# First mixer of a two-block transformer kernel: eight modulation chunks multiplied and summed on VectorE, with TensorE summing over partitions only

## What is computed

```python
mod = (silu(c) @ w_mod + b_mod).reshape(bsz, 6, 1024)      # for x
mc = (silu(c_ctx) @ w_mod + b_mod).reshape(6, 1024)        # for ctx, only mc[0] and mc[1] are used
hc = modulate(rmsnorm(ctx, g_mix), mc[0], mc[1])           # -> forget gates, values -> two start states
h = modulate(rmsnorm(x, g_mix), mod[:, 0], mod[:, 1])
mix_x = token_mixers(h @ w_in, ..., start states)          # gated linear attention + spatial gating
x = x + mod[:, 2] * mix_x
h2 = modulate(rmsnorm(x, g_ffn), mod[:, 3], mod[:, 4])
x = x + mod[:, 5] * swiglu(h2, w_up, w_down)
```

## Time and profile before

| | |
|---|---|
| runs shown, us | 1447.14, 1448.66, 1449.80 |
| median, us | 1448.66 |
| span of the profiled execution, us | 1447.1 |
| busy share of the span: TensorE, VectorE, ScalarE | 98%, 59%, 53% |
| granted TensorE clock, mean | 0.996 |
| bytes moved by DMA, mean rate | 268.39 MB, 185 GB/s |

### The profile page before, as it was taken

One profiled execution on the slowest core, in us unless ns is written; L12 is line 12 of the kernel. 1 busy time (PEld: TensorE's weight loads), 2 busy tenths in 40 slices (PEclk: granted clock), 3 DMA queues, 4 the chain that ended last, 5 costly groups with the idle time before them and its releaser, 6 DMA issues.

```text
span 1447.1 us, 19624 instructions
## 1 busy us (share of the span) xinstructions
PE 1420.6 (98%) x8042; PEld 1195.6 (83%) x8042; DVE 860.0 (59%) x1205; ACT 766.7 (53%) x1126; POOL 37.1 (3%) x72
## 2 busy tenths in 40 slices
PE   6999999999999999999999999999999999999998
PEld 5898889978888788888997888888888889888886
DVE  3628766875554755556576655557555475765553
ACT  4535355464453654446685655546545376754542
POOL 0000000000000000000241000000000000000000
PEclk9999999999999999999999999999999999999999
DMA  9537666555555556555534555565655551365552
GB/s 386 206 133 277 224 235 211 178 185 182 184 188 189 198 183 186 189 189 192 172 118 146 180 187 189 185 201 182 188 185 182 188 181 60 128 185 184 186 189 88
DMA packets 70074, 268.39 MB, mean 185 GB/s; under 512 B 7776, under 2 KB 8032, under 8 KB 66400
## 3 DMA queue, kind: packets, MB, share of 16 engines
q1 hardware_dynamic: 67968, 261.23, 53.5%
q10 hardware_dynamic: 2016, 5.90, 1.5%
HBM read 266.05 MB, written 1.05 MB: 185 GB/s over the span
## 4 chain that ended last, share of the span: by engine, by line
PE 92%; DVE 3%; ACT 2%; DMA 1%; issue 1%; SPq 0%; POOL 0%; ACTq 0%
PE PS L726 25%; PE PS L742 14%; PE PS L744 14%; PE PS L743 14%; PE PS L379 5%; PE PS L380 4%; PE PS L381 4%; PE PS L710 2%; PE PS L481 1%; PE PS L413 1%; DMA MC<-in_mod 1%; PE PS L414 1%; PE PS L415 1%; DVE WL L1701 1%; PE PS L1001 1%
## 5 line engine op out<-in xcount | busy, mean ns | idle before, releaser
L1701 DVE TENSOR_TENSOR WL<-RAW,WH 128x1024 fp32r<-128x1024 f32 (+1 forms) x440 | 533.8, 1223 | 282.4 <-ACT WH L1101 281.0
L1101 ACT ACTIVATE WH<-RAW 128x1024 fp32r<-128x1024 f32 (+1 forms) x440 | 452.2, 1054 | 263.0 <-DMA RAW<-in_up 134.2
L742 PE MATMUL PS<-WH,XH 128*128 128x512 f32 (+1 forms) x928 | 381.6, 411 | 2.8 <-DVE XL L2150 2.2
L744 PE MATMUL PS<-WH,XL 128*128 128x512 f32 (+1 forms) x928 | 362.8, 391 | 0.0
L743 PE MATMUL PS<-WL,XH 128*128 128x512 f32 (+1 forms) x928 | 362.5, 391 | 0.0
L742 PEld LDWEIGHTS PS<-WH,XH 128*128 128x128 f32 x928 | 174.7, 188 | 52.4 <-DVE XL L2150 5.9
L744 PEld LDWEIGHTS PS<-WH,XL 128*128 128x128 f32 x928 | 174.5, 188 | 37.2
L743 PEld LDWEIGHTS PS<-WL,XH 128*128 128x128 f32 x928 | 175.5, 189 | 27.7
L726 PE MATMUL PS<-WH,GH 128*128 128x512 f32 x440 | 137.8, 394 | 0.0
L726 PE MATMUL PS<-WL,GH 128*128 128x512 f32 x440 | 135.8, 390 | 0.0
L726 PE MATMUL PS<-WH,GL 128*128 128x512 f32 x440 | 135.8, 390 | 0.0
(11 more groups left out here) (351 smaller groups left out, 1832.9 us busy)
## 6 DMA issues: line engine op xcount, KB each, us to landing
RAW<-in_up SPq DMA_DIRECT2D x220, 512.0 KB, 3.6
RAW<-in_down SPq DMA_DIRECT2D x110, 512.0 KB, 3.3
RAW<-in_win SPq DMA_DIRECT2D x36, 512.0 KB, 4.8
RAW<-in_mod SPq DMA_DIRECT2D x16, 1024.0 KB, 6.7
MC<-in_mod SPq DMA_DIRECT2D x8, 1024.0 KB, 11.7
RAW<-in_sbqk SPq DMA_DIRECT2D x16, 512.0 KB, 5.0
GROW<-in_grow ACTq DMA_DIRECT2D x9, 512.0 KB, 4.7
RAW<-in_fg SPq DMA_DIRECT2D x8, 512.0 KB, 8.8
```

The costliest lines, as they stand in the source:

```text
L742: e.matmul(o_[:, 0:n], l, w[:, s], start=(k == 0), stop=False, skip_group_check=True)
L744: m = e.matmul(o_[:, 0:n], ll, w[:, s], start=False, stop=(k == KD - 1), skip_group_check=True)
L1101: e.activation(WH[s][:, 0:c], RAW[s][:, 0:c], ACT.Copy).then_inc(*sig("hi", j))
L1701: e.tensor_tensor(WL[s][:, 0:c], RAW[s][:, 0:c], WH[s][:, 0:c].bitcast(F32), ALU.subtract).then_inc(*sig("lo", j))
```

## The change

Chunks 8 to 15 of the modulation leave the weight plan and the slots. They are loaded in four pairs (8 and 9, 10 and 11, 12 and 13, 14 and 15; `EARLY`) into one buffer ME of 16 KB for each partition. VectorE multiplies the eight row blocks of a pair by the condition, one scalar for each partition, and adds them up in a tile MA of 512 columns (`early_sums`). TensorE sums over the partitions (`early_rows`): one matmul with a matrix of ones for the pairs 8 and 10, four matmuls with slices of MA as the stationary operand for the pairs 12 and 14. VectorE adds the bias (`early_added`). SP loads pair 0 after the gate's chunks and the others after the chunks 14, 17 and 19, each after the sums of the pair before it. ScalarE waits for the last sums before it loads ROW and WST, which lie where ME is. The places of the remaining chunks 16 to 23 among the projections change with it.

```diff
-    nxt = 8
+    late = {11: (16, 17), 13: (18, 19), 15: (20,), 17: (21,), 19: (22,), 20: (23,)}
     for i in range(10, 22):
-        n = 2 if i < 14 else 1
-        plan += [("mod", nxt + z, 2048) for z in range(n)]
-        nxt += n
+        plan += [("mod", n, 2048) for n in late.get(i, ())]
         plan += [("win", 2 * i + z, 1024) for z in range(2)]
...
+        ME = ph("ME", 64, [P, 2, 2048])
+        MA = Ring([ph(f"MA{i}", 60 + 2 * i, [P, 2, T]) for i in range(2)])
+        EARLY = (8, 10, 12, 14)
...
+            def early_rows(i):
+
+                b, empty = bank(("modt", i), ("mod", i))
+                ma = MA.of(("ma", i))
+                pe.wait_ge(*at("ma", i))
+                pe.wait_ge(*empty)
+                if i // 4 == 2:
+                    m = e.matmul(b[:, :], ONE, ma[:, :, :], start=True, stop=True)
+                else:
+                    for t in range(4):
+                        m = e.matmul(b[:, 2 * t:2 * t + 2], ma[:, t // 2, t % 2 * P:t % 2 * P + P], ONE[:, 0:2],
+                                     start=True, stop=True)
+                m.then_inc(*sig("modt", i))
...
-            for c in range(2):
-                token_chunk("win", 4 + c, ("vt", 0, c), ("vc", 0, c), HH, HL, at("hl", 7))
-                token_chunk("win", 4 + c, ("vt", 1, c), ("vc", 1, c), HCH, HCL, at("hcl", 7))
-            for c in range(2):
-                pair("win", 6 + c, ("pl", "Q", c), ("plc", "Q", c), HH, HL, at("hl", 7))
+            token_chunk("win", 4, ("vt", 0, 0), ("vc", 0, 0), HH, HL, at("hl", 7))
+            early_rows(8)
+            token_chunk("win", 4, ("vt", 1, 0), ("vc", 1, 0), HCH, HCL, at("hcl", 7))
+            early_rows(10)
+            token_chunk("win", 5, ("vt", 0, 1), ("vc", 0, 1), HH, HL, at("hl", 7))
+            token_chunk("win", 5, ("vt", 1, 1), ("vc", 1, 1), HCH, HCL, at("hcl", 7))
+            early_rows(12)
+            pair("win", 6, ("pl", "Q", 0), ("plc", "Q", 0), HH, HL, at("hl", 7))
+            pair("win", 7, ("pl", "Q", 1), ("plc", "Q", 1), HH, HL, at("hl", 7))
+            early_rows(14)
...
-            mods(8)
             plain("OG", 0, 10)
-            mods(9)
             gla_scores(0)
-            mods(10)
+            mods(16)
             gla_states(0)
-            mods(11)
+            mods(17)
             plain("OG", 1, 11)
             gla_out(0)
-            mods(12)
             plain("UU", 0, 12)
-            mods(13)
             gla_scores(1)
-            mods(14)
+            mods(18)
             gla_states(1)
-            mods(15)
+            mods(19)
             plain("UU", 1, 13)
...
+            ac.wait_ge(*at("ma", 14))
             for i in range(3):
                 e.dma_start(ROW[:, i, :], a["rows"][i:i + 1, :].to_broadcast([P, 512])).then_inc(s_row, 16)
             e.dma_start(WST[:, :, :], a["wst"]).then_inc(s_row, 16)
...
+            def early_sums(p):
+
+                i = EARLY[p]
+                ma, before = MA.take(("ma", i), ("modt", i))
+                dv.wait_ge(s_early, 32 * (p + 1))
+                dv.wait_ge(*at("act", "silc"))
+                dv.wait_ge(*after(before))
+                for k in range(KD):
+                    w, s = ME[:, :, k * T:(k + 1) * T], SILC[:, k, 0:1]
+                    if k == 0:
+                        e.tensor_scalar(ma[:, :, :], w, s, None, ALU.mult).then_inc(*sig("dve", "ma", i, k))
+                        continue
+                    dv.wait_ge(*at("dve", "ma", i, k - 1))
+                    m = e.scalar_tensor_tensor(ma[:, :, :], w, s, ma[:, :, :], ALU.mult, ALU.add)
+                    m.then_inc(*(sig("dve", "ma", i, k) if k < KD - 1 else sig("ma", i)))
...
             split(9)
+            early_sums(0)
             for src, dst in enumerate((FX, FC)):
...
                 split(14 + src)
-            for c in range(2):
-                split_to("win", 4 + c)
+            early_sums(1)
+            early_added(0)
+            early_sums(2)
+            early_added(1)
+            split_to("win", 4)
+            early_sums(3)
+            split_to("win", 5)
+            early_added(2)
             dv.wait_ge(*at("act", "ln c"))
...
+            def early(p):
+                if p:
+                    sp.wait_ge(*at("ma", EARLY[p - 1]))
+                for z in range(2):
+                    e.dma_start(ME[:, z, :], a["mod"][EARLY[p] + z]).then_inc(s_early, 16)
+
+            early(0)
             for j in range(KD, len(plan)):
                 weights(j)
+                if j in (14, 17, 19):
+                    early({14: 1, 17: 2, 19: 3}[j])
```

More of the change, by code:

```diff
@@ L614, in pe_program @@
                 m.then_inc(*sig("s0", dr))
-            mods(8)
             plain("OG", 0, 10)
-            mods(9)
             gla_scores(0)
-            mods(10)
+            mods(16)
             gla_states(0)
-            mods(11)
+            mods(17)
             plain("OG", 1, 11)
             gla_out(0)
-            mods(12)
             plain("UU", 0, 12)
-            mods(13)
             gla_scores(1)
-            mods(14)
+            mods(18)
             gla_states(1)
-            mods(15)
+            mods(19)
             plain("UU", 1, 13)
-            mods(16)
             gla_out(1)
             plain("GA", 0, 14)
-            mods(17)
+            mods(20)
             plain("GA", 1, 15)
-            mods(18)
             plain("GA", 2, 16)
@@ L648, in pe_program @@
                 m.then_inc(*sig("ob", z))
-            mods(19)
+            mods(21)
             plain("GA", 3, 17)
-            mods(20)
             plain("GB", 0, 18)
@@ L661, in pe_program @@
                 m.then_inc(*sig("sg", g))
-            mods(21)
+            mods(22)
             plain("GB", 1, 19)
-            mods(22)
+            mods(23)
             plain("GB", 2, 20)
-            mods(23)
             plain("GB", 3, 21)
@@ L1746, in mods, with early_added @@
                     split_to("mod", i)
+            def early_sums(p):
[12 more added lines that the diff above has]
+                    m.then_inc(*(sig("dve", "ma", i, k) if k < KD - 1 else sig("ma", i)))
+            def early_added(p):
+                i = EARLY[p]
+                dv.wait_ge(*at("modt", i))
+                b = BANK.of(("modt", i))
+                if i // 4 == 2:
+                    c = slice(i % 4 * T, i % 4 * T + 2 * T)
+                    dv.wait_ge(s_grow[0], 16)
+                    e.tensor_tensor(GROW[0][:, c], b[:, :], GROW[0][:, c], ALU.add).then_inc(*sig("mod", i))
+                else:
+                    e.tensor_tensor(MOD[:, 2 * i:2 * i + 4, :], four(b[:, 0:8]),
+                                    SM[:, S_BMOD + 2 * i:S_BMOD + 2 * i + 4].unsqueeze(2).to_broadcast([P, 4, 2]),
+                                    ALU.add).then_inc(*sig("mod", i))
             def scale_of(name, dst, gcol, mcol, which, n):
@@ L1860, in dve_program @@
             plain(7)
+            early_added(3)
             dv.wait_ge(*at("vt", 1, 1))
```

26 lines of the change are left out of this document (9 added, 17 removed).

## The result

The changed kernel takes 1455.97 us in the median (1455.02 to 1456.45); the kernel before, run beside it on the same chip, 1448.76. The ratio is 1.0049, with a 95% interval of 1.0036 to 1.0061: 7.2 us slower. The profiled execution spans 1453.8 us against 1447.1, 6.7 more.

The account below looks back on a forecast made before the run. TensorE, busy 98% of the span, bounds the kernel; transposes 16.1 us late, less 12.7 of removed matmuls, plus 4.0 of later waits, make +7.4: 1448.66 becomes 1456 us, range 1450 to 1461.

Parts of the forecast that it names:

- TensorE's early rows: Four row sums added on TensorE ahead of the transposes L602: 3.6 us, free if TensorE waits there anyhow.
- VectorE's sums: One multiplication and seven multiply-and-adds on VectorE for each pair of chunks: 6.05 us, 5.4 to 6.6 as bounds.
- Rival C: VectorE's multiply-and-adds take 0.27 us a step, so the loaded pairs finish sooner: -3.3 us, 1445; chance 0.06.
- Chunk 15 behind 2 MB: Chunk 15 queues on SP behind pair 1's load; its low half ends at about 81.9, 82.5 at most.
- The reload: Refilling the single buffer ME after a pair's sums: 8.3 us plus 0.1 for hand-overs, twice on the chain.
- Rival B: Quick refills of ME, 5.3 us each: +1.4 us, 1450, not to be told from no change; chance 0.12.
- ScalarE's queue: ScalarE's loads of ROW and WST wait for the last sums at 116.9, putting the logarithm behind them at 120.1.
- The stop at chunk 17: TensorE idles 8.3 us, from 119.6 to 127.9, in the first value chunk, waiting for chunk 17's low half.
- The clock at the stop: After the idle wait at chunk 17 TensorE runs at half clock for 3.3 us, costing 1.65 us.
- rival A: TensorE's clock stays up through the wait at chunk 17: L602 ends 15.0 late, +6.3 us, 1455; shares chance 0.82.
- The waits after them: After the transposes L602, TensorE waits for KD and KT in both directions: together 4.0 us (2 to 6).
- rival D: Clock falls in short waits too, or a refill of ME takes 9.5 us: +10 to +12, 1460; shares chance 0.82.

## Why the prediction was right, point by point

The forecast, 1456 us and slower, was met with 1455.97. Part of that closeness is luck, since two terms were off in opposite directions.

- **TensorE's loss of work.** By the ledger 12.0 to 12.9 us, 12.3 in the mean; forecast 12.7. Right.
- **TensorE's early rows.** In the two-buffer kernel, where TensorE is hardly waiting ahead of the transposes, and which stands level with the kernel before at 56 us, these start 4.3 us late, of which 0.5 is the wait for the low half. The rest, 3.8, is the early rows with the hand-overs around them; I had 3.6, hidden in the stop. Right.
- **VectorE's sums.** 0.49 and 5.48 us, and 5.9 from a pair's start to the start of what follows it; I had 6.05, and 5.4 to 6.6 as bounds. Rival C, with a step of 0.27 us, is out: seven steps take 5.48, 0.78 each.
- **Chunk 15 behind 2 MB.** Its low half ended at 80.91 + 1.23 = 82.1 in the profiled execution (81.9 forecast). In the other kernels with early pairs it ended between 82.1 and 84.2, in six of ten beyond my bound of 82.5: right here, with too narrow a bound.
- **The reload: mis-sized.** I took 8.3 and 0.1 from a pair of chunks at 125.56. From the first issue to the start of the sums it took 95.26 - 88.08 = 7.2 and 108.65 - 101.28 = 7.4. Two of them make the last sum 2.2 us earlier than said, 114.65 instead of 116.9, and the logarithm with it, 117.80 instead of 120.1; TensorE's wait of 2 us at the last early rows has all but gone. The estimate of 6.8 us from the Trainium skill ("DMA: Bandwidth & Descriptors", Anatomy of one DMA) was nearer than my row: a bound of 7.3 stood in the range, and 8.3 was the wrong end to take it from. Rival B, with 5.3, is out.
- **ScalarE's queue.** From the last sum to the logarithm 117.80 - 114.65 = 3.15 us, forecast 3.2. Right; and the run with the loads behind the logarithm shows that the whole wait on ScalarE is worth 3 to 4 us of the time and not more.
- **The stop at chunk 17.** 8.08 us (forecast 8.3), ended by VectorE's low half. Right.
- **The clock at the stop.** It was at 0.50 from 122 to 128, and had begun to rise between 128 and 130, some 3 us after work resumed. 36 matmuls and their switches took 131.35 - 125.68 = 5.67 us, against 4.54 in the two-buffer kernel (117.67 to 122.21, at a clock of 1.00): 1.1 us, forecast 1.65. Right in kind; rival A is out. Even a clock that stays up wouldn't give all of it back: Pc's second half was ready at 128.93 + 2.37 = 131.30 and no earlier, and with the matmuls in the stop the transposes did wait for it.
- **The transposes.** 13.5 us late and not 16.1: 2.2 from the reloads, the rest from the 36 matmuls (5.67 us, forecast 4.4 + 1.65).
- **The waits after them: mis-sized.** I said 4.0: KD 1.8 and 1.0, KT 0.6 and 0.6. KD came at 1.99 and 1.13, the second KT at 0.57; the first KT wait vanished where TensorE ran at half clock, and in the two runs with the same places and no fall there (loads behind the logarithm, matmuls in the stop the second time) it is there, with 0.57. But I missed two things: the wait of 1.17 us for MR at 211.22, as VectorE copies chunk 20 only behind the normalisation block and two low halves (at 210.74), and the second fall of the clock from 152 to 156 us, 1.7 us, which I had as rival D. Together 6.6 instead of 4.0.
- **The sum.** -2.6 at the transposes and +2.6 behind them. The mechanism was right and the total close because these cancel; by the sizes that the runs showed, the same sum is +7.4.

What stays open: why the clock falls after a wait of 2.0 us in one execution and not in another. The two-buffer kernel's profile shows the fall after such a wait, the kernel with the loads behind the logarithm has one as long and no fall; the kernel before has a fall at 1174 that others with the same wait don't have. Open is also why these reloads took 7.2 to 7.4 us and the pair at 125.56 took 8.6.

## What to carry to other kernels

Work moved to an idle engine is only as early as its data. When the moved work needs a buffer, write down buffer free, load, compute for each turn and see what stands behind the last turn, on every queue that waits for it. And when work leaves the bound engine, look at what it was covering: here some 12 us of matmuls were a gain only in so far as the waits that they had stood in front of were filled with something else, and moving the remaining pieces there paid only once each one's own follow-up work had been moved too.

## What the runs showed of the hardware

- The granted clock fell after short waits too. In the changed kernel TensorE worked from 125.7 on and stood still for 1.99 us ahead of 151.41; the clock was at 0.73 from 152 to 153 and at 0.50 from 153 to 155. My sum had a fall only behind the stop of 8 us. The kernel before does it too, at 1174, after a wait of 1.85 us.
- A fall isn't the same in every execution of one program. The moved-chunk kernel with two buffers took 1446 us in four executions at a clock of 0.999 or 1.000, and 1450.8 to 1454.9 in eight at 0.992 to 0.994. The stretch at 0.50 was some 3 us long in the two-buffer kernel (from 143 to 146) and 10 in the one with half the chunks (from 141 to 151).
- Two loads of 1 MB each, issued together, were there 7.2 and 7.4 us after the first issue (the DMA engines' busy share was 0.00 in the two microseconds before the first of these reloads); in the kernel before, a pair at 125.56 took 8.6.
